# Recurrence of a two-block transformer kernel: the first chunk products of two of the four chains are issued in the input stages

## The chip, the cores and the metric

The kernel runs on one core of one Trainium2 chip, in one launch. The metric is the device time of the launch in microseconds (us). Five engines work side by side and meet at semaphores: TensorE (PE in the profile, with its weight loads as PEld), VectorE (DVE), ScalarE (ACT), GpSimd (POOL) and the queue of SyncE (SP), which issues most transfers.

## The reference, cut to what matters

Two transformer blocks over 256 tokens of width 1024. The second block holds a gated linear recurrence over 8 heads of size 64, run forward and backward in time, once over a context of 256 tokens (only the last state is needed) and once over the tokens themselves:

```
def step(S, inp):
    w_t, k_t, v_t, a_t, b_t = inp[:5]
    sa = jnp.einsum('bhij,bhj->bhi', S, a_t)
    S = S * w_t[:, :, None, :] + sa[..., None] * b_t[:, :, None, :] + v_t[..., None] * k_t[:, :, None, :]
    y = jnp.einsum('bhij,bhj->bhi', S, inp[5]) if emit else None
    return S, y
```

After it come a merge with a convolution branch, and a mixture of 16 experts whose weights are most of the bytes that the kernel reads.

## The kernel before, in words

The kernel does not step through the tokens. It cuts the 256 tokens into 8 chunks of 32 (`CH`), and solves each chunk with small matrix products. `recurrence_phase` runs twice: for the context (names begin with `rc`, `ctx_only` is true) and for the tokens (`rl`). Each run has two directions, d = 0 and d = 1, and for each direction two stages, one behind the other: `recurrence_inputs` and `recurrence_chunks`. That makes four pairs of stages: rc0, rc1, rl0, rl1. Each stage is a block of its own: every engine waits at its end for the others, and GpSimd clears the semaphores of the stage, one after another, before it goes on.

**The input stage** makes the scaled factors. DVE writes `ar[:, :, 0]` (L2683), `bk[:, :, 0]` (L2688), `bk[:, :, 1]` (L2691), and for the tokens `ar[:, :, 1]` (L2698). `ebk[:, 0]` is made on POOL (L2644) and `ebk[:, 1]` on DVE (L2695). One semaphore, `ready`, counts the three that are to be transposed: 1 for `ar` from DVE, 2 for `ebk[:, 0]` from POOL, 3 for `ebk[:, 1]` from DVE. DVE waits for `ready` to be 2 before it makes `ebk[:, 1]`, so that the count has one meaning. PE transposes each in two groups of four 128x128 tiles (L2605), `j` counting the tensors (0 is `v`), into two PSUM banks in turn, and ACT copies each group out (L2631). PE also does a matrix product for a later stage in pieces (L2097, `LateModulation`), and where d is 1 it carries the states of the direction before (`States`, L3070 to L3084), with DVE adding between them (L3100). Behind DVE's products, POOL keeps the keys for the tokens (L2649, L2651).

**The chunk stage** works on four chains, q = 0 to 3, each half of the tokens and half of the heads. `order()` goes through 13 rounds r, and in each through the four chains. In round 0, PE makes the raw products of a chain: 32 matmul instructions for the context and 48 for the tokens, each 64 rows deep with 32 columns of weights (L2831, L2833, L2835, L2837). A profile shows each of them as two matmul records and two weight loads, because they are float32. DVE then masks them (L3006) and spreads them (L3008), ACT copies four corners (L2929) and writes `off` (L2934), into buffers that POOL has set to zero (L2957, L2958). Rounds 1 and later multiply, spread and combine. PE starts round 1 of a chain when DVE and ACT have done its round 0.

PSUM has eight banks. Chain q uses banks 2q and 2q + 1. In the input stage the small products of the decay and the rate use banks 2 to 5 (L2582, L2584), the transposes banks 6 and 7 where d is 0 and 2 and 3 where d is 1, the states banks 0, 1 and 6, and the piecewise product bank 0 or 7.

Of the kernel before, what the change touches and what calls it, by code (L numbers as in the profile page):

```python
# [8 lines left out]
P = 128  # L9
# [2526 lines left out]


def recurrence_inputs(nc, g, I, z, ar, bk, tok, pc, store, part, st, ctx_only, name, d):

# [3 lines left out]
    with ExitStack() as ctx:  # L2543
# [34 lines left out]
        @block.tensor  # L2578
        def _(pe):
            pe.wait_ge(g.lora_in, 32 * lora_loads)  # L2580
            for c in range(PAIRS):
                nc.tensor.matmul(ps[:, 2 + c // 2, T * (c % 2):T * (c % 2) + T], g.lora[0:64, P * c:P * c + P],  # L2582
                                 z[0:64, 12, :], start=True, stop=True).then_inc(S["lora_w"], 1)
                mm = nc.tensor.matmul(ps[:, 4 + c // 2, T * (c % 2):T * (c % 2) + T], g.lora[64:P, P * c:P * c + P],  # L2584
                                      z[64:P, 12, :], start=True, stop=True)
            mm.then_inc(S["lora"], 1)
            if d:
                for n in range(NCH):
                    before.pe_step(pe, n)
                    for k in range(2 * n, min(2 * n + 2, KC)):  # L2590
                        late.pe_step(pe, k)

            q = 0
            for j in range(d, 4):
                if j == 1 and d == 0:
                    for k in range(KC):
                        late.pe_step(pe, k)
                if j:
                    pe.wait_ge(S["ready"], j)
                for t in range(TT):  # L2600
                    if q >= 2:
                        pe.wait_ge(S["tokcopy"], q - 1)
                    for c in range(PAIRS):
                        src = (v_[:, c], ar[:, c, 0], ebk[:, 0, c], ebk[:, 1, c])[j][:, P * t:P * t + P]
                        mm = nc.tensor.transpose(ps[:, turn0 + q % 2, P * c:P * c + P], src, g.ident[:])  # L2605
                    mm.then_inc(S["tokturn"], 1)
                    q += 1
# [28 lines left out]
        def _(pool):  # L2636
            p_ = nc.gpsimd
            for c in range(PAIRS):
# [5 lines left out]
            p_.tensor_tensor(chunked(ebk[:, 0]), chunked(bk[:, :, 0, :]), pc[:].unsqueeze(3).to_broadcast([P, PAIRS, NCH, CH]),  # L2644
                             ALU.mult).then_inc(S["ready"], 1)
            if not ctx_only:
# [8 lines left out]
        def _(dve):  # L2655
# [12 lines left out]
            for c in range(PAIRS):  # L2668
                dve.wait_ge(S["log"], c + 1)
                ins = v.tensor_tensor_scan(onward(cum[:, c, :]), g.restart[:], onward(ld[:, c, :]), 0.0, ALU.mult, ALU.add)  # L2670
                if c == 1:
# [18 lines left out]
            dve.wait_ge(S["keys"], 1)  # L2690
            ch(v.tensor_tensor(bk[:, :, 1, :], keys[:], shrunk[:], ALU.mult))  # L2691
            move_state()
            dve.wait_ge(S["exp"], 3)
            dve.wait_ge(S["ready"], 2)
            v.tensor_tensor(chunked(ebk[:, 1]), chunked(bk[:, :, 1, :]), pc[:].unsqueeze(3).to_broadcast([P, PAIRS, NCH, CH]),  # L2695
                            ALU.mult).then_inc(S["ready"], 1)
            if not ctx_only:
                ch(v.tensor_tensor(ar[:, :, 1, :], r, grown[:], ALU.mult))  # L2698
            if d and not ctx_only:
# [8 lines left out]
def recurrence_chunks(nc, g, ar, bk, tok, pc, store, part, ctx_only, name, d):  # L2708
# [6 lines left out]
    with ExitStack() as ctx:  # L2715
# [57 lines left out]
        def g2c(q):  # L2773
            return pair[:, q, 1]

        def order():
            for r in range(CHUNK_ROUNDS):
                for q in range(len(its)):
                    yield q, r

        def group(i):
            return slice(CH * i, CH * i + CH)
# [25 lines left out]
        def _(pe):  # L2808
# [9 lines left out]
            for q, r in order():  # L2818
                (t, h4), out = its[q], bank(q, r)
                by_dve, by_act = S[f"by_dve{q}"], S[f"by_act{q}"]  # L2820
                if r == 0:
                    for k in range(2):
                        for kind in range(2 if ctx_only else 3):
                            for c in range(4):
                                for e in range(2):
                                    half, pr = slice(HD * e, HD * e + HD), 2 * h4 + k
                                    tok_c = slice(P * t + CH * c, P * t + CH * c + CH)
                                    a, bb = ar[half, pr, :, tok_c], bk[half, pr, :, tok_c]
                                    out = ps[group(c), 2 * q + e, 256 * k:256 * k + n_raw]
                                    if kind == 0:  # L2830
                                        mm = mm_(out[:, 0:64], a[:, 0], bb[:, 0:2], start=True, stop=True)  # L2831
                                    elif ctx_only:
                                        mm = mm_(out[:, 64:96], bb[:, 0], a[:, 0], start=True, stop=True)  # L2833
                                    elif kind == 1:
                                        mm = mm_(out[:, 64:128], bb[:, 0], a[:, 0:2], start=True, stop=True)  # L2835
                                    else:
                                        mm = mm_(out[:, 128:160], bb[:, 1], a[:, 1], start=True, stop=True)  # L2837
                elif r == 1:
# [36 lines left out]
                elif r == 5:  # L2875
                    pe.wait_ge(by_dve, FACTOR)
                    if not ctx_only:
                        pe.wait_ge(S["joined"], q + 1)
                    for hs in range(4):
# [10 lines left out]
                elif r == 8:  # L2890
                    pe.wait_ge(by_dve, FTIL)
                    pe.wait_ge(S["read_out"], q + 1)
                    for hs in range(4):
                        mm = by_pairs(out, hs, read_out(q)[:, hs], ftil(q)[:, hs])
                else:
# [4 lines left out]
                    else:  # L2900
                        pe.wait_ge(S[f"pe{q}"], r)
                    for k in range(2):
# [13 lines left out]
        def _(act):  # L2916
# [3 lines left out]
            for q, r in order():  # L2920
                (t, h4), done = its[q], S[f"by_act{q}"]
                if r in (4, 7, 8, 9, 11, 12):
                    continue
                act.wait_ge(S[f"pe{q}"], r + 1)
                if r == 0:
                    act.wait_ge(S["zeros"], q + 1)
                    act.wait_ge(S[f"by_dve{q}"], RAW)
# [26 lines left out]
        def _(pool):  # L2954
            tt, copy, zero = nc.gpsimd.tensor_tensor, nc.gpsimd.tensor_copy, nc.gpsimd.memset
            for q in range(NQ):
                zero(off[:, q], 0.0)  # L2957
# [6 lines left out]
            def join(q):  # L2964
                t, h4 = its[q]
                pool.wait_ge(S[f"pe{q}"], 3)
                kt = tok[:, 1, t, 256 * h4:256 * h4 + 256].rearrange("p (k e n) -> p e k n", k=2, e=2)
                copy(f1(q)[:, :, 0:HD].rearrange("p (e k) n -> p e k n", e=2), kt)
                copy(f1(q)[:, :, HD:wide], raw[:, q, :, 96:128]).then_inc(S["joined"], 1)

            for q in range(NQ):
                expand(q)
            if not ctx_only:
                for q in range(NQ):
                    join(q)
            for q in range(NQ):
                pool.wait_ge(S[f"pe{q}"], 5)
                tt(in_halves(read_out(q)), twice(raw[:, q, :, CH:2 * CH]), own_half, ALU.mult).then_inc(S["read_out"], 1)
# [3 lines left out]
            if not ctx_only:  # L2982
                for q, (t, h4) in enumerate(its):
                    pool.wait_ge(S[f"by_dve{q}"], G2)
# [6 lines left out]
        def _(dve):  # L2991
# [8 lines left out]
            for q, r in order():  # L3000
                (t, h4), done = its[q], S[f"by_dve{q}"]
                if r in (5, 6, 9, 10, 11):
                    continue
                dve.wait_ge(S[f"pe{q}"], r + 1)
                if r == 0:
# [10 lines left out]
                elif r == 2:  # L3016
                    spread_low(q, r).then_inc(done, 1)
                    dve.wait_ge(S[f"by_act{q}"], HIGH + 1)
                    dve.wait_ge(S["expanded"], q + 1)
                    dve.wait_ge(S["minus"], 1)  # L3020
# [894 lines left out]
```

## Time and profile before

| What | Value |
|---|---|
| Median of 3 runs | 2251.73 us (2250.79 to 2252.65) |
| Span of the profiled execution | 2252.5 us |
| Instructions | 36461 |
| PE busy | 1746.6 us (78%) |
| PE weight loads busy | 1172.5 us (52%) |
| DVE busy | 826.5 us (37%) |
| ACT busy | 652.2 us (29%) |
| POOL busy | 230.2 us (10%) |
| Read from the chip's main memory | 584.88 MB |

The span is the time from the first to the last instruction of one profiled execution; only the span is shown for that execution, and it lies within the three times. Busy shares are averages over a whole program with very different stages, so they say little about the recurrence. The four pairs of stages lie at these times of the span: rc0 from 801 to 858 us, rc1 from 858 to 918, rl0 from 1035 to 1099, rl1 from 1099 to 1171.

### The profile page before, as it was taken

How to read it: one execution, taken by the hardware profiler on the slowest of the kernel's cores; microseconds unless marked ns; L12 is line 12 of the kernel's file. 1: busy time of each engine (PE TensorE's matmuls, PEld its weight loads, DVE VectorE, ACT ScalarE, POOL GpSimd, SP SyncE). 2: the span in 40 equal slices, each digit the busy share in tenths (PEclk: the TensorE clock that was granted, in tenths of full speed). 3: DMA queues.
4: the chain of work that ended last, by engine and by line, in shares of the span. 5: the costliest groups of instructions: out<-in, count | busy, mean ns of one | idle time of the engine just before them, and what ended most of it. 6: DMA issues, size and time to landing. Idle time of an engine off the chain costs nothing. (4 is left out here: it accounts for less than half of the span.)

```text
span 2252.5 us, 36461 instructions
## 1 busy us (share of the span) xinstructions
PE 1746.6 (78%) x15950; PEld 1172.5 (52%) x15950; DVE 826.5 (37%) x1187; ACT 652.2 (29%) x1053; POOL 230.2 (10%) x222
## 2 busy tenths in 40 slices
PE   7999988979999977897889976556566666565654
PEld 7997986867878855796779741111111111111111
DVE  5654445765755666675656540000000000000001
ACT  5434445564423455444453320000000000000001
POOL 0100014430121032002330000000000000000000
PEclk9999998999999989897979988887778877778787
DMA  7654652235855522253215579999999999999997
GB/s 234 188 187 150 206 161 64 88 129 189 279 162 191 182 92 78 73 178 100 66 41 206 204 279 428 429 428 428 428 428 428 428 428 428 428 428 428 427 427 305
DMA packets 181906, 588.39 MB, mean 261 GB/s; under 512 B 11363, under 2 KB 144166, under 8 KB 156918
## 3 DMA queue, kind: packets, MB, share of 16 engines
q1 hardware_dynamic: 180550, 585.32, 67.6%
q8 instruction: 126, 2.06, 0.4%
q10 hardware_dynamic: 1200, 0.76, 0.1%
q14 instruction: 30, 0.25, 0.0%
HBM read 584.88 MB, written 1.17 MB: 260 GB/s over the span
## 5 line engine op out<-in xcount | busy, mean ns | idle before, releaser
L193 DVE TENSOR_TENSOR split_lo<-ring,split_hi 128x2048 fp32r<-128x2048 f32 x127 | 295.8, 2331 | 193.6 <-ACT split_hi L186 192.9
L3659 PE MATMUL ps<-ex_ring,ex_xe 128*32 128x512 f32 x1440 | 233.5, 783 | 157.0 <-DMA ex_ring<-in_exp_w 157.0
L3740 DVE TENSOR_TENSOR ex_hid<-ps,ex_silu 128x512 f32<-128x512 f32 x16 | 11.1, 692 | 863.1 <-PE ps L3659 863.1
L221 PE MATMUL ps<-xt_hi,split_hi 128*128 128x256 f32 x984 | 284.4, 289 | 13.0 <-DVE xt_lo L350 5.3
L186 ACT CAST split_hi<-ring 128x2048 fp32r<-128x2048 f32 x127 | 240.4, 1897 | 144.1 <-PE ps L223 123.5
L222 PE MATMUL ps<-xt_lo,split_hi 128*128 128x256 f32 x984 | 279.2, 284 | 0.0
L223 PE MATMUL ps<-xt_hi,split_lo 128*128 128x256 f32 x984 | 279.0, 284 | 0.0
L3659 PEld LDWEIGHTS ps<-ex_ring,ex_xe 128*32 128x32 f32 x1440 | 45.1, 128 | 342.0 <-DMA ex_ring<-in_exp_w 246.7
L221 PEld LDWEIGHTS ps<-xt_hi,split_hi 128*128 128x128 f32 x984 | 188.5, 192 | 24.9 <-issue 14.3
L222 PEld LDWEIGHTS ps<-xt_lo,split_hi 128*128 128x128 f32 x984 | 188.5, 192 | 1.2 <-issue 1.2
L221 PE MATMUL ps<-split_hi,xt_hi 128*128 128x256 f32 (+1 forms) x560 | 175.6, 314 | 16.7 <-DVE split_lo L193 7.1
L223 PEld LDWEIGHTS ps<-xt_hi,split_lo 128*128 128x128 f32 x984 | 188.4, 191 | 0.0
L222 PE MATMUL ps<-split_lo,xt_hi 128*128 128x256 f32 (+1 forms) x560 | 174.4, 312 | 0.0
L223 PE MATMUL ps<-split_hi,xt_lo 128*128 128x256 f32 (+1 forms) x560 | 173.8, 310 | 0.0
L3681 PE MATMUL ps<-ex_ring,ex_ht 128*32 128x512 f32 x688 | 112.1, 783 | 72.7 <-DMA ex_ring<-in_exp_w 66.0
L221 PEld LDWEIGHTS ps<-split_hi,xt_hi 128*128 128x128 f32 x560 | 107.3, 192 | 25.2 <-DVE split_lo L193 5.8
L223 PEld LDWEIGHTS ps<-split_hi,xt_lo 128*128 128x128 f32 x560 | 107.1, 191 | 6.3
L222 PEld LDWEIGHTS ps<-split_lo,xt_hi 128*128 128x128 f32 x560 | 107.3, 192 | 5.8
L3659 PE MATMUL ps<-ring,ex_xe 128*32 128x512 f32 x416 | 65.5, 762 | 47.2 <-DMA ring<-in_exp_w 45.6
L3681 PEld LDWEIGHTS ps<-ex_ring,ex_ht 128*32 128x32 f32 x688 | 21.6, 129 | 149.4 <-DMA ex_ring<-in_exp_w 98.0
L3700 ACT COPY ex_wselt<-ps 128x256 f32<-128x256 f32 x16 | 6.0, 373 | 294.8 <-PE ps L3665 294.8
L3698 ACT ACTIVATE ex_silu<-ps 128x512 f32<-128x512 f32 x16 | 9.6, 597 | 276.3 <-PE ps L3659 276.3
(766 smaller groups left out, 2811.5 us busy)
## 6 DMA issues: line engine op xcount, KB each, us to landing
ex_ring<-in_exp_w SPq DMA_DIRECT2D x133, 2048.0 KB, 46.0
ring<-in_exp_w SPq DMA_DIRECT2D x39, 2048.0 KB, 46.0
ring<-in_w_in SPq DMA_DIRECT2D x55, 1024.0 KB, 5.3
ex_late<-in_exp_w SPq DMA_DIRECT2D x18, 2048.0 KB, 46.2
ring<-in_ffn_w_gate SPq DMA_DIRECT2D x22, 1024.0 KB, 6.0
ring<-in_ffn_w_up SPq DMA_DIRECT2D x22, 1024.0 KB, 5.5
ring<-in_ffn_w_down SPq DMA_DIRECT2D x22, 1024.0 KB, 4.9
ring<-in_mod_w SPq DMA_DIRECT2D x16, 1024.0 KB, 6.5
```

What stands on the lines that cost most here:

```text
L186: nc.scalar.copy(g.whi[:, s % H, 0:n], g.ring[:, i % R, 0:n]).then_inc(g.hi_done, 1)
L193: eng.tensor_tensor(g.wlo[:, s % H, 0:n], g.ring[:, i % R, 0:n], g.whi[:, s % H, 0:n].bitcast(F32), ALU.subtract).then_inc(g.tiles_split, 1)
L221: nc.tensor.matmul(out, lhs[0], rhs[0], start=start, stop=False, skip_group_check=shared)
L222: nc.tensor.matmul(out, lhs[0], rhs[1], start=False, stop=False, skip_group_check=shared)
L223: return nc.tensor.matmul(out, lhs[1], rhs[0], start=False, stop=stop, skip_group_check=shared)
L3659: mm = mm_(ps[32 * q:32 * q + 32, 4 + u, :], xe[:, k], w[:, 512 * q:512 * q + 512], start=k == 0, stop=k == KC - 1)
L3681: mm = mm_(ps[32 * q:32 * q + 32, 7, :], ht[:, 2 * (k % 2) + h, CAP * f:CAP * f + CAP], w[:, h, 512 * n:512 * n + 512], start=k == 0, stop ...
L3698: nc.scalar.activation(silu[:], ps[:, 4, :], ACT.Silu).then_inc(S["silu"], 1)
L3700: nc.scalar.copy(wselt[:], ps[:, 6, 0:T]).then_inc(S["wselt"], 1)
L3740: v.tensor_tensor(hid[:], ps[:, 5, :], silu[:], ALU.mult).then_inc(S["hid"], 1)
```

## The change

Four things are changed.

1. The raw products of round 0 become a function, `first_products`. For two of the four chains (1 and 2 where d is 0, 2 and 3 where d is 1) it is called in the input stage, before the transposes of `ebk[:, 0]` and of `ebk[:, 1]`, and no longer in the chunk stage. Their banks are free of the input stage's own work by then.
2. A new semaphore, `factors`, is raised once both halves of `bk` (and for the tokens both of `ar`) are written. PE waits for it before the first of these calls. For the tokens, DVE makes `ar[:, :, 1]` before `ebk[:, 1]` and not after it.
3. `ready` is split in three, so that DVE makes `ebk[:, 1]` without waiting for POOL's `ebk[:, 0]`.
4. In the chunk stage the two early chains come first in each round, on every engine, and the waits count their PE rounds from round 1.

```diff
+EARLY = {0: (1, 2), 1: (2, 3)}
+def first_products(nc, g, ar, bk, ctx_only, q):
...
     (in recurrence_inputs, tensor)
+                if j >= 2:
+                    if j == 2:
+                        pe.wait_ge(S["factors"], 1)
+                        pe.wait_ge(S["log"], PAIRS)
+                        pe.wait_ge(S["rate"], PAIRS)
+                    elif d:
+                        pe.wait_ge(S["state"], before.moves + 1)
+                        pe.wait_ge(g.mod_copied, late.n + 1)
+                    first_products(nc, g, ar, bk, ctx_only, EARLY[d][j - 2])
                 if j:
-                    pe.wait_ge(S["ready"], j)
+                    pe.wait_ge(S[("", "ready", "ready_b", "ready_k")[j]], 1)
...
     (in recurrence_inputs, vector)
             dve.wait_ge(S["keys"], 1)
-            ch(v.tensor_tensor(bk[:, :, 1, :], keys[:], shrunk[:], ALU.mult))
+            if not ctx_only:
+                ch.add(v.tensor_tensor(bk[:, :, 1, :], keys[:], shrunk[:], ALU.mult))
+                v.tensor_tensor(ar[:, :, 1, :], r, grown[:], ALU.mult).then_inc(S["factors"], 1)
+            else:
+                ins = v.tensor_tensor(bk[:, :, 1, :], keys[:], shrunk[:], ALU.mult)
+                ins.then_inc(S["factors"], 1)
             move_state()
+            dve.wait_ge(S["factors"], 1)
             dve.wait_ge(S["exp"], 3)
-            dve.wait_ge(S["ready"], 2)
             v.tensor_tensor(chunked(ebk[:, 1]), chunked(bk[:, :, 1, :]), pc[:].unsqueeze(3).to_broadcast([P, PAIRS, NCH, CH]),
-                            ALU.mult).then_inc(S["ready"], 1)
-            if not ctx_only:
-                ch(v.tensor_tensor(ar[:, :, 1, :], r, grown[:], ALU.mult))
+                            ALU.mult).then_inc(S["ready_k"], 1)
...
     (in recurrence_chunks)
+        early = EARLY[d]
+        chains = [*early, *(q for q in range(NQ) if q not in early)]
         def order():
             for r in range(CHUNK_ROUNDS):
-                for q in range(len(its)):
+                for q in chains:
                     yield q, r
...
                 if r == 0:
+                    if q in early:
+                        continue
+                    mm = first_products(nc, g, ar, bk, ctx_only, q)
```

The body of `first_products` is the loop of round 0, moved without an edit. The lines in brackets say where a piece stands.

## Rows read from the trace of the kernel before

**Rows 1.** Page, part 4: the chain that ended last, share of the span by engine.
```profile
DMA 37%; PE 3%; DVE 0%; ACT 0%; SPq 0%; issue 0%; DVEq 0%
```

**Rows 2.** Windows: from:to, length, busy (records) by engine, PE first, clock, DMA share, GB/s.
```profile
1055.50:1100.00 44.50, 34.97 (x1250) 31.44 (x1252) 25.56 (x53) 22.54 (x66) 19.12 (x32) 0.81 0.05 14
...
1059.60:1061.65 2.05, 2.03 (x128) 0.50 0.03 8
...
1063.10:1065.70 2.60, 2.60 (x128) 0.50 0.02 6
...
821.75:823.70 1.95, 1.91 (x176) 1.00 1.10 347
```

**Rows 3.** Timeline of PE, rl0: start, us, operation, and in brackets idle before and releaser.
```profile
1050.06 4.03 PE L2605 MATMUL ps<-ident,rl0i_ebk 128*128 128x128 f32 x16 [2.07 <-POOL rl0i_ebk L2644]
1055.53 0.47 PE L2831 MATMUL ps<-rl_bk,rl_ar 64*32 64x64 f32 x16 [1.45 <-PEq L2543]
...
1059.62 0.21 PE L2837 MATMUL ps<-rl_ar,rl_bk 64*32 64x32 f32 x1 [1.96 <-issue]
```

**Rows 4.** Timeline of ACT, first copies of round 0 and of round 1, rl0.
```profile
1058.03 1.22 ACT L2929 COPY rl0c_both<-rl0c_raw 32x128 f32<-32x128 f32 x4 [1.89 <-DVE rl0c_raw L3006]
...
1067.91 0.74 ACT L2939 COPY rl0c_both<-ps 32x256 f32<-32x256 f32 x2
```

**Rows 5.** Timeline of ACT, the same in rc0, rc1 and rl1.
```profile
823.53 1.22 ACT L2929 COPY rc0c_both<-rc0c_raw 32x128 f32<-32x128 f32 x4 [1.14 <-POOL rc0c_both L2958]
...
830.92 4.57 ACT L2939 COPY rc0c_both<-ps 32x256 f32<-32x256 f32 x12
...
882.67 1.22 ACT L2929 COPY rc1c_both<-rc1c_raw 32x128 f32<-32x128 f32 x4 [1.28 <-POOL rc1c_both L2958]
...
889.36 5.39 ACT L2939 COPY rc1c_both<-ps 32x256 f32<-32x256 f32 x14
...
1139.76 0.74 ACT L2939 COPY rl1c_both<-ps 32x256 f32<-32x256 f32 x2
```

**Rows 6.** Timeline of POOL, second half of the first chain's zeros in rl0.
```profile
1057.02 0.53 POOL L2958 MEMSET rl0c_both<- 128x512 f32 x1
```

**Rows 7.** Timeline of DVE and of POOL, input stage of rl0.
```profile
1047.02 1.22 DVE L2691 TENSOR_TENSOR rl_bk<-rl0i_keys,rl0i_shrunk 128x1024 f32<-128x1024 f32 x1
1050.14 1.92 DVE L2695 TENSOR_TENSOR rl0i_ebk<-rl_bk,rl_pc 128x1024 f32<-128x1024 f32 x1 [1.91 <-POOL rl0i_ebk L2644]
...
1047.18 2.82 POOL L2644 TENSOR_TENSOR rl0i_ebk<-rl_bk,rl_pc 128x1024 f32<-128x1024 f32 x1 [3.68 <-DVE rl_bk L2688]
```

**Rows 8.** Timeline of DVE, of POOL and of PE, input stage of rl1.
```profile
1118.96 2.52 DVE L2691 TENSOR_TENSOR rl_bk<-rl1i_keys,rl1i_shrunk 128x1024 f32<-128x1024 f32 x1
...
1120.37 3.35 POOL L2651 TENSOR_TENSOR kmod_y<-kmod_y,rl1i_keys 128x1024 f32<-128x1024 f32 x1
...
1124.85 1.09 PE L2605 MATMUL ps<-ident,rl1i_ebk 128*128 128x128 f32 x8 [1.54 <-DVE rl1i_ebk L2695]
1127.76 0.47 PE L2831 MATMUL ps<-rl_bk,rl_ar 64*32 64x64 f32 x16 [1.82 <-PEq L2543]
```

**Rows 9.** Timelines of PE in rc0, then of DVE and PE in rc1, input stages.
```profile
816.50 3.79 PE L2605 MATMUL ps<-ident,rc0i_ebk 128*128 128x128 f32 x16 [2.82 <-POOL rc0i_ebk L2644]
...
873.67 2.83 DVE L2691 TENSOR_TENSOR rc_bk<-rc1i_keys,rc1i_shrunk 128x1024 f32<-128x1024 f32 x1
...
876.06 3.28 PE L2605 MATMUL ps<-ident,rc1i_ebk 128*128 128x128 f32 x16
```

**Rows 10.** Timeline of DVE and POOL elsewhere: two products in a row against one of POOL.
```profile
500.92 3.59 DVE L193 TENSOR_TENSOR split_lo<-ring,split_hi 128x2048 fp32r<-128x2048 f32 x1
...
499.95 2.41 POOL L1521 TENSOR_TENSOR proj<-proj 128x1024 f32<-128x1024 f32 x1 [26.19 <-DVE proj L1543]
```

**Rows 11.** Timeline of DVE and POOL in rl1: two scans in a row against one operation of POOL.
```profile
1104.46 1.29 DVE L2670 TENSOR_TENSOR_SCAN rl1i_cum<-restart,rl1i_ld 128x256 f32<-128x256 f32 x2
...
1104.77 1.18 POOL L2640 TENSOR_SCALAR rl1i_keys<-rl1i_av,vb,one_minus_ka 128x256 f32<-128x256 f32 x1 [10.49 <-ACT rl1i_av L2617]
```

## Prediction before the run

> **What bounds the kernel now.** I read the page first. The chain that ended last is 37% DMA and 3% PE [rows 1]: from the experts on, the kernel waits for weights. That stream starts only after the recurrence, the merge and the router, and its loads are issued as those stages free their buffers. So a microsecond won or lost in the recurrence moves the stream by as much, and I carry it over at full value.
>
> Then I read the timelines of each engine in the four pairs of stages, because shares of busy time say nothing about stages that wait for one another. Three things stand out.
>
> First, PE in round 0 of a chunk stage is not held by a semaphore but by "issue". In rl0 it stood still for 1.96 us until 1059.62, then ran exactly 128 records, stood still, and ran 128 again [rows 2, 3]. The runs of 128 begin 3.5 us apart (1059.60 and 1063.10). One matmul record goes with one weight load, so a run is 256 instructions. The reading: instructions arrive in blocks of 256, one is executed while the next one is there, and the block after that is asked for when a block is finished; it takes 3.5 us or more. Where the matmuls are small, PE eats a block in 2.05 us at the half clock (0.50) and then waits. The Trainium skill (Runtime: NRT & Kernel Launch, Instruction fetch mechanics) also has blocks of 256 instructions, but gives PE room for 2048 and calls the crossing mostly hidden. By that the stalls would not be there, and my sum would be about 1 us lower, since I count one such stall in rl1. The trace disagrees: PE stops after every 128 records.
>
> Second, round 0 sets the start of everything else. ACT copies the corners of all four chains before it may touch round 1. In rc1 these copies ran without a gap, from 882.67 to 889.36 [rows 5], 6.7 us for four chains. In rl0 they took from 1058.03 to 1067.91 [rows 4], since each waited for raw products.
>
> Third, DVE and POOL hold each other up. POOL's `ebk` product took 2.82 us in rl0 beside a DVE product that started before it [rows 7]; DVE's product took 2.52 us in rl1 instead of 1.22 [rows 7, 8].
>
> **What the chunk stages gain.** The removed work is round 0 of two chains, out of the way before the stage begins. DVE can mask them at once, and the two chains left are made meanwhile. What sets the end of round 0 is then ACT: its start plus 6.7 us. Its start needs zeros from POOL, which in rl0 came at 1057.02 + 0.53 = 1057.55, that is 2.0 us after the stage began at 1055.53 [rows 3, 6]. POOL clears three semaphores more in each input stage (`factors`, `ready_b`, `ready_k`). Their clears are not in the rows; POOL needs less than 1.5 us from the start of the stage to its zeros, for 14 semaphores, so three more cost at most 0.3 us; I take 0.2.
> - rl0: before, round 1 on ACT began 1067.91 - 1055.53 = 12.4 us into the stage. After: 2.0 + 0.1 + 0.2 + 6.7 = 9.0. Gain 3.4.
> - rl1: before 1139.76 - 1127.76 = 12.0 [rows 5, 8]; after 9.0. Gain 3.0.
> - rc0: before, 830.92 - 821.8 = 9.1, with ACT already released by POOL at 823.53 [rows 2, 5]. After: 1.7 + 0.2 + 6.7 = 8.6. Gain 0.5.
> - rc1: ACT was already without a gap behind POOL's zeros [rows 5]. Nothing to gain; the clears cost 0.2.
>
> Sum of gains: 3.4 + 3.0 + 0.5 - 0.2 = 6.7 us. From round 1 on every instruction stands at the same place in PE's stream, so I take the rest as shifted and unchanged.
>
> **What the input stages lose.** PE stands idle before `ebk[:, 0]` only: 2.07 us in rl0, 2.82 in rc0 [rows 3, 9]. The call before `ebk[:, 1]` has no such cover, since the transposes run in one piece of four groups. The price of a call: 64 records for the context, 96 for the tokens, at 2.05 / 128 = 16 ns a record at the half clock, 1.95 / 176 = 11 ns at full [rows 2]. So 0.7 to 1.0 us, and 1.05 to 1.5 us. Two groups of transposes took 1.09 us at full clock (rl1) and 4.03 / 2 = 2.0 us in rl0 [rows 3, 8]. After the last transpose, copy and barrier took 1055.53 - 1054.09 = 1.44 us.
> - rc0: the first call runs while PE waits for POOL and is free. The second costs 0.7 to 1.0. If the call keeps the clock up, the transposes, 3.79 us here [rows 9], would go in 2.2, a gain. Bounds -0.9 and +1.0; I take +0.8, nearest to the rows.
> - rc1: before, the transposes started at 876.06 and ended at 879.34. Now the first call waits for `bk`, ready at 873.67 + 2.83 = 876.50 [rows 9]. Then 0.7, 1.1, 0.7, 1.1: end at 880.1, at the half clock in part 881. ACT's copies, which paced the transposes before, hide behind the calls. +0.8 to +1.7; I take +1.2.
> - rl0: the call needs `ar[:, :, 1]` too, which DVE now makes right behind `bk[:, :, 1]`, in the time when POOL's `ebk` product waits for the shared path. Who goes first? Elsewhere DVE ran, straight behind another product, one over 2048 columns in 3.59 us, where 1024 columns take 1.22 alone [rows 7], so some 2.4 were due; a product of POOL that was issued before it took 2.41 us and ended 1.4 us into it [rows 10]: POOL got in between. So POOL runs until 1050.0, DVE until 1051.1, and the call starts at 1051.15 and not at 1049.4. Then call, two groups, call, two groups: 1.5 + 2.0 + 1.5 + 2.0 = 7.0 at the half clock, end 1058.15 against 1054.09, +4.1. At full clock it is 1.05 + 1.1, then the second call meets a block that was asked for at 1051.5 and comes 3.7 us later, then 0.4 and 1.1: 1056.8, +2.7. PE will be denser than before, so I take +3.5.
> - rl1: `bk` is ready at 1121.48. POOL's `kmod` product has waited since 1120.37 and ran until 1123.72 [rows 8]; by the same order `ar[:, :, 1]` runs after it, until 1124.8. PE has nothing else to do by then and stands still. Call 1.05, two groups 1.1, then the second call stalls for its block (asked for at 1125.4, there at 1129.1), 0.2, and two groups 1.1 to 2.0: end 1130.4 to 1131.3. Before: 1125.94. The stage ended then 1.8 us after it, as DVE copied outputs, and now 1.44. +4.1 to +5.0; I take +4.4.
>
> Sum of losses: 0.8 + 1.2 + 3.5 + 4.4 = 9.9 us. Dropping DVE's wait for POOL gains nothing by itself: both want the same path, and PE is not waiting for `ebk[:, 1]` any more.
>
> **Sum.** 9.9 - 6.7 = +3.2 us: rc0 +0.3, rc1 +1.4, rl0 +0.1, rl1 +1.4. The profiled execution spans 2252.5 us, within the three runs, so on the median 2251.7 + 3.2 = 2254.9 us. A difference of under 0.2% (4.5 us) is about what a measurement of this kernel can't tell from none.
>
> **Rivals.**
> - *DVE keeps the path between two products in a row.* Two scans did: a POOL operation issued during the first took 1.18 us and ended after the second, which was not slowed (the two took 1.29) [rows 11]. Then `factors` comes at 1049.4 and 1122.6. rl0 costs 1.5 us less, rl1 2.5 less: -0.8, 2250.9 us. The Trainium skill (SBUF — State Buffer, two separate sides) says that whichever starts first holds the pair for the whole instruction, which agrees with rows 7 and leaves open who is next. Chance 0.20.
> - *Instruction blocks bind the whole chunk stage (the faster side).* A chunk stage for the tokens has some 1250 records, 9.8 blocks, at 3.5 us 34 us of its 44. If the blocks set the pace past round 1, moving 1 block out of each context stage and 1.5 out of each token stage saves 2 x 3.5 + 2 x 5.2 = 17.5 us instead of 6.7: 2251.7 + 9.9 - 17.5 = 2244 us. It decides from the point where PE waits for "issue" in late rounds; in rl0 the waits of that kind that I found are in round 0 and the first of round 1. Chance 0.10.
> - *Blocks come late while weights are loaded.* Weights of later stages load during the input stages; where such a load still ran, the DMA share was 1.10 [rows 2]. The fetches inside the input stages were hidden, so their length there is unknown. If one takes 6 us instead of 3.7, each second call ends some 2 us later: +4 to +5, 2259 us. Chance 0.15.
>
> **How the numbers follow.** The forecast has 0.55; its own range is 2251 to 2258, with a third of it above the 0.2% line. Slower: 0.18 from it and 0.14 of the late blocks, 0.32. Faster: the block rival, 0.10. Same: 0.58. The range 2249 to 2260 leaves out the block rival and the far end of the late ones.
>
> **What would show it.** In the changed kernel: PE's wait for `factors` ends at DVE's `ar` product in rl0 and rl1, some 3 us after `bk` starts in rl0; a wait on "issue" inside the second call of rl1; input stages longer by about 1, 1, 3.5 and 4.5 us; ACT's copies of round 0 without a gap, 6.7 us in all four; chunk stages for the tokens shorter by about 3 us. Wrong if DVE's `ar` product is not held up, if the clock rises in the input stages, or if late rounds of the chunk stages shrink too.

## The result

The changed kernel is slower: 2261.34 us median of 20 runs, against 2255.33 us of the kernel before in 20 runs beside them. The two medians lie 6.0 us apart; the ratio of the fast runs, which leaves out two of the kernel before at 4029 and 5836 us, is 1.0035 [1.0027, 1.0043], some 8 us. The profiled executions say much the same: span 2259.8 us against 2252.5, +7.3. The forecast was +3.2 us, 2254.9 (from a median of three runs that lay 3.6 us below that of the twenty), with a range to 2260, which the median passes by 1.3 us. The direction was right and the size, by the ratio, less than half of what came.

I cut each pair of stages at three events of ACT: its first activation of the input stage, the start of the chunk stage, and its first copy of round 1. "Rest" runs from there to the next stage. In us, worked out from ACT's timeline, one profiled execution each:

| | input stage: before, after, forecast | round 0: before, after, forecast | rest: before, after, forecast |
|---|---|---|---|
| rc0 | 18.24, 18.85: +0.6, +0.8 | 9.16, 8.63: -0.5, -0.5 | 29.73, 30.49: +0.8, 0 |
| rc1 | 20.11, 20.94: +0.8, +1.2 | 8.60, 8.77: +0.2, +0.2 | 27.40, 27.92: +0.5, 0 |
| rl0 | 18.39, 24.32: **+5.9, +3.5** | 12.40, 8.98: -3.4, -3.4 | 33.85, 34.13: +0.3, 0 |
| rl1 | 25.97, 31.95: **+6.0, +4.4** | 12.03, 8.91: -3.1, -3.0 | 31.68, 32.20: +0.5, 0 |

From the start of rc0 to the merge the kernel took 367.92 us before and 375.76 after, +7.8. It is made up of +13.3 in the input stages, -6.9 in round 0, +2.1 in the rests, and -0.7 in the work between rc1 and rl0. After the merge both need the same time (1081.1 and 1081.3).

### The profile page after: what moved, and what is told of

Its sections match the earlier page's. It is cut to its first block and busy times, and to the rows that moved or that the text cites. A ratio compares the mean times of both kernels' runs of the same rounds, so it can differ in the third digit from the quotient of the medians.

```text
span 2259.8 us, 36476 instructions
## 1 busy us (share of the span) xinstructions
PE 1752.3 (78%) x15950; PEld 1177.2 (52%) x15950; DVE 829.6 (37%) x1187; ACT 651.3 (29%) x1053; POOL 231.0 (10%) x222
## 5 line engine op out<-in xcount | busy, mean ns | idle before, releaser
L221 PE MATMUL ps<-xt_hi,split_hi 128*128 128x256 f32 x984 | 284.7, 289 | 13.3 <-DVE xt_lo L350 5.6
L221 PEld LDWEIGHTS ps<-xt_hi,split_hi 128*128 128x128 f32 x984 | 188.6, 192 | 25.2 <-issue 14.4
L3716 PE MATMUL ps<-ex_ring,ex_ht 128*32 128x512 f32 x688 | 116.9, 813 | 77.9 <-DMA ex_ring<-in_exp_w 73.2
```

The costliest lines, as they stand in the source:

```text
L221: nc.tensor.matmul(out, lhs[0], rhs[0], start=start, stop=False, skip_group_check=shared)
L3716: mm = mm_(ps[32 * q:32 * q + 32, 7, :], ht[:, 2 * (k % 2) + h, CAP * f:CAP * f + CAP], w[:, h, 512 * n:512 * n + 512], start=k == 0, stop ...
```

## The profile after

The chain that ended last still waits for weights, as in [rows 1]:

```profile
DMA 37%; PE 3%; DVE 0%; ACT 0%; issue 0%; DVEq 0%
```

DVE and POOL in the input stage of rl0 (start, us, instruction, idle before and releaser), which answer to [rows 7]:

```profile
1047.64 1.22 DVE L2727 TENSOR_TENSOR rl_bk<-rl0i_keys,rl0i_shrunk 128x1024 f32<-128x1024 f32 x1
1048.78 2.94 DVE L2728 TENSOR_TENSOR rl_ar<-z,rl0i_grown 128x1024 f32<-128x1024 f32 x1
1051.75 1.94 DVE L2735 TENSOR_TENSOR rl0i_ebk<-rl_bk,rl_pc 128x1024 f32<-128x1024 f32 x1
...
1047.82 2.82 POOL L2679 TENSOR_TENSOR rl0i_ebk<-rl_bk,rl_pc 128x1024 f32<-128x1024 f32 x1 [3.68 <-DVE rl_bk L2723]
```

DVE's `ar[:, :, 1]` was issued behind `bk[:, :, 1]` and took 2.94 us in place of 1.22: POOL's product, which had waited since 1047.82, went in between. `factors` came at 1051.72. The stages ahead had moved all of this by 0.62 us (1047.64 against 1047.02), so it came at 1051.1 on the clock of before, which is the forecast.

PE in the same stage, the answer to [rows 3]:

```profile
1051.77 0.47 PE L2554 MATMUL ps<-rl_bk,rl_ar 64*32 64x64 f32 x16 [4.03 <-DVE rl_ar L2728]
...
1053.21 1.96 PE L2640 MATMUL ps<-ident,rl0i_ebk 128*128 128x128 f32 x8
1055.10 0.34 PE L2554 MATMUL ps<-rl_bk,rl_ar 64*32 64x64 f32 x16
...
1055.60 0.28 PE L2554 MATMUL ps<-rl_bk,rl_ar 64*32 64x64 f32 x4
1058.33 0.28 PE L2554 MATMUL ps<-rl_bk,rl_ar 64*32 64x64 f32 x5 [2.45 <-issue]
...
1058.99 1.97 PE L2640 MATMUL ps<-ident,rl0i_ebk 128*128 128x128 f32 x8
1062.38 0.47 PE L2554 MATMUL ps<-rl_bk,rl_ar 64*32 64x64 f32 x16 [1.42 <-PEq L2569]
```

The first call takes 1.4 us, its two groups of transposes 1.9. The second call gets through 55 records and stops for "issue", that is for instructions. Counted back from the stop, 128 records are those 55, the 8 transposes, and 65 of the 96 of the first call, so the block in use began at its 32nd record, at about 1052.2. By the prediction's reading the next block was asked for then. It was there at 1058.33: 6.1 us, where the forecast had 3.7. All lengths of a fetch in this document are counted this way. The windows (length, busy and records of PE, PEld, DVE, ACT, POOL, granted clock, DMA share, GB/s) show what else went on:

```profile
1051.80:1053.20 1.40, 1.40 (x96) 1.35 (x96) 1.40 (x1) 0.00 (x0) 0.81 (x1) 0.50 1.10 347
1053.20:1055.20 2.00, 2.00 (x27) 1.67 (x27) 0.49 (x1) 0.59 (x1) 0.00 (x0) 0.54 1.10 349
1055.20:1058.50 3.30, 0.85 (x75) 0.70 (x82) 0.00 (x0) 0.59 (x1) 0.00 (x0) 0.99 1.01 326
1058.50:1061.00 2.50, 2.45 (x49) 1.99 (x35) 0.00 (x0) 0.60 (x2) 0.00 (x0) 0.50 0.06 20
```

Weights of a later stage load at 326 to 349 GB/s until just before the block is there. In rl1 there is the same stop, with a difference:

```profile
1128.13 0.35 PE L2554 MATMUL ps<-rl_bk,rl_ar 64*32 64x64 f32 x16 [2.92 <-DVE rl_ar L2728]
...
1129.18 1.09 PE L2640 MATMUL ps<-ident,rl1i_ebk 128*128 128x128 f32 x8
...
1133.60 0.31 PE L2558 MATMUL ps<-rl_ar,rl_bk 64*32 64x64 f32 x1 [2.42 <-issue]
...
1134.05 1.97 PE L2640 MATMUL ps<-ident,rl1i_ebk 128*128 128x128 f32 x8
```

```profile
1128.70:1131.30 2.60, 2.48 (x146) 2.10 (x132) 1.96 (x5) 1.07 (x2) 0.00 (x0) 1.00 1.09 342
1131.30:1133.60 2.30, 0.00 (x1) 0.00 (x1) 0.00 (x0) 0.00 (x0) 0.00 (x0) 0.99 0.05 16
```

By the same count (78 records of the second call, 8 transposes, 42 of the first call) the block in use began at about 1128.7, and the next took 4.9 us. Here the loads were over at about 1131.3, and the block came 2.3 us after that. PE came out of the wait, did a fifth of a call, and had its last two groups at the half clock (1.97 us, against 1.09 for the two before).

The chunk stage of rl0 on ACT, the answer to [rows 4]:

```profile
1064.64 1.22 ACT L2963 COPY rl0c_both<-rl0c_raw 32x128 f32<-32x128 f32 x4 [1.66 <-POOL rl0c_both L2992]
1065.88 0.52 ACT L2968 ACTIVATE rl0c_off<-ps,halves 128x64 f32<-128x64 f32 x2
1066.29 1.20 ACT L2963 COPY rl0c_both<-rl0c_raw 32x128 f32<-32x128 f32 x4
...
1071.33 0.74 ACT L2973 COPY rl0c_both<-ps 32x256 f32<-32x256 f32 x2
```

ACT is released by POOL's zeros, 2.26 us into the stage (1064.64 - 1062.38; forecast 2.0 + 0.1 + 0.2), and then copies all four chains without a gap, 6.69 us (forecast 6.7).

## The experiments

Each kernel was timed in five rounds against the kernel before on the same chip, 6 to 12 executions against 22 to 35; ratios are against that, and the row "after" repeats the result. The columns of stages are, for rl0 and rl1, input stage / round 0 / rest, in us, each from one profiled execution:

| kernel | ratio | rl0 | rl1 | rc0 to merge |
|---|---|---|---|---|
| before | 1 | 18.4 / 12.4 / 33.9 | 26.0 / 12.0 / 31.7 | 367.9 |
| after | 1.0035 [1.0027, 1.0043] | 24.3 / 9.0 / 34.1 | 32.0 / 8.9 / 32.2 | 375.8 |
| e1_loads_later | 1.0049 [1.0035, 1.0063] | 21.5 / 9.0 / 34.0 | 30.4 / 8.9 / 34.9 | 377.4 |
| e2_none_early | 1.0016 [1.0005, 1.0028] | 19.1 / 12.3 / 33.8 | 29.4 / 11.5 / 31.7 | 371.4 |
| e3_context_only | 1.0028 [1.0016, 1.0039] | 19.2 / 12.7 / 34.0 | 27.1 / 12.3 / 32.0 | 372.2 |
| e4_tokens_only | 1.0022 [1.0011, 1.0033] | 24.1 / 9.0 / 33.8 | 31.7 / 8.9 / 32.0 | 372.6 |
| e5_one_call | 0.9995 [0.9985, 1.0005] | 19.6 / 9.7 / 33.3 | 29.5 / 8.9 / 31.9 | 367.2 |
| e6_ar_first | 1.0030 [1.0020, 1.0040] | 21.9 / 9.0 / 33.9 | 32.7 / 8.9 / 32.0 | 372.9 |
| e7_tokens_one_free | 0.9989 [0.9977, 1.0001] | 18.9 / 9.0 / 33.6 | 27.0 / 9.8 / 32.5 | 365.6 |
| e8_before_keys_last | 0.9994 [0.9982, 1.0007] | 18.0 / 12.4 / 33.3 | 25.2 / 11.5 / 32.3 | 366.2 |
| e9_two_calls_free | 1.0022 [1.0012, 1.0032] | 22.8 / 9.0 / 33.6 | 33.8 / 8.9 / 31.7 | 372.4 |
| e10_one_call_free | 0.9995 [0.9986, 1.0004] | 18.9 / 9.0 / 33.4 | 26.8 / 9.8 / 32.0 | 363.6 |
| e11_before_loads_later | 1.0078 [1.0063, 1.0092] | 18.1 / 16.3 / 35.0 | 26.3 / 15.3 / 33.1 | 382.7 |

### e1_loads_later: is the block late because of the weights?

The changed kernel, with the loads of the late weight tiles issued in the following chunk stage and not in the input stage:

```diff
-            late.load_next(sp)                 (input stage, sync)
+        load_tiles(g, sp, ... + 4 + R)         (chunk stage, sync)
```

> The changed kernel, with SyncE's loads of the next four weight tiles moved from the input stages into the chunk stages that follow. Theory 1 (a block of instructions comes late because it queues behind weight loads): PE's wait on issue inside the second call of rl0 and rl1, 2.7 us each in the changed kernel, shrinks to 1 us or less, the input stages of rl0 and rl1 end some 2 us earlier each, and the time falls by 3 to 5 us against the changed kernel, to +2 to +5 us against the kernel before. Theory 2 (a fetch takes its 6 us whatever else is moved): the waits stay at 2.5 us and more, and the time stays at about +8 us.

The input stages got shorter, by 2.9 us in rl0 and 1.6 in rl1. In rl0 the second call starts at 1056.73 and its transposes follow at 1058.17, 1.44 us later, with no wait on "issue" in it:

```profile
1056.73 0.47 PE L2554 MATMUL ps<-rl_bk,rl_ar 64*32 64x64 f32 x16
...
1058.17 1.15 PE L2640 MATMUL ps<-ident,rl0i_ebk 128*128 128x128 f32 x8
```

PE's instructions are those of the changed kernel, so a block ends at the same record. In rl0 that is the 56th of the second call, some 3.7 us after the block began, and the next one was there. In rl1 it is the 79th, and PE's weight loads stop there for only 0.27 us:

```profile
1130.90 0.22 PEld L2558 LDWEIGHTS ps<-rl_ar,rl_bk 64*32 64x32 f32 x13
1131.38 0.10 PEld L2558 LDWEIGHTS ps<-rl_ar,rl_bk 64*32 64x32 f32 x1 [0.27 <-issue]
```

The block in use had begun at 1127.90, so this fetch took 3.5 us, and 4.9 with the loads beside it. Theory 1 holds for the stages: a block comes late because of the loads. The time did not fall with it, as theory 1 had it: it is 1.0049, some 3 us above the changed kernel (the intervals overlap) and not 3 to 5 below. The rest of the chunk stages grew by 1.9 us (rc0), 0.7 (rc1) and 2.7 (rl1) over the changed kernel, where the loads now run beside the chunk stage's blocks: one fetch took 7.3 us in rl0 and one 6.8 in rl1. I had not seen that the loads must be somewhere.

### e11_before_loads_later: the same move in the kernel before

> The kernel before with the loads of the late weight tiles moved from the input to the following chunk stage. Theory (a block of instructions comes late while weights load): the input stages, where fetches lie under other waits, stay within 0.5 us, and the chunk stages grow by 1 to 3 us in rc0 and rl1 as they did with the same move in the changed kernel; time 2255 to 2258 us. Rival (the chunk stages grew for another reason in that version): chunk stages within 0.5 us, time the same as before.

The stage changed, and the size was wrong: input stages within 0.7 us, chunk stages 2.0 (rc0) and 4.4 us (rc1) longer, those of the tokens 5.0 (rl0) and 4.7 us (rl1), there mostly in round 0. The kernel was 0.78% slower, some 17.6 us and not 2 to 5. PE in round 0 of rl0:

```profile
1062.54 0.32 PE L2831 MATMUL ps<-rl_bk,rl_ar 64*32 64x64 f32 x13 [1.42 <-PEq L2543]
1066.76 0.21 PE L2837 MATMUL ps<-rl_ar,rl_bk 64*32 64x32 f32 x1 [2.68 <-issue]
1073.24 0.26 PE L2835 MATMUL ps<-rl_ar,rl_bk 64*32 64x64 f32 x1 [4.46 <-issue]
```

and what the window of that stretch holds:

```profile
1063.00:1073.00 10.00, 3.11 (x238) 2.79 (x234) 2.84 (x4) 3.55 (x13) 3.82 (x10) 0.59 0.99 319
```

The same code as in [rows 2, 3], whose runs of 128 records began 3.5 us apart, has them 6.5 us apart (1066.76, 1073.24) when weights load at 319 GB/s. This is the price of a block by itself, without any of the change: 3.5 us in a quiet stage, 6.5 beside weight loads. Over the thirteen traces, the fetches inside one stage that PE had to wait for took 2.9 to 4.4 us with the DMA share under 0.1 and 5.8 to 7.3 us with it above 0.9. Some that run over the end of an input stage don't fit: the one after the stop in rl1 of the changed kernel took 7.2 us, from 1133.60 to 1140.81, at a DMA share of 0.01. Why is open.

### e2, e3 and e4: the change in parts

e2_none_early keeps DVE's order and the split `ready` and issues no call early; e3_context_only has the calls of rc0 and rc1, e4_tokens_only those of rl0 and rl1.

```diff
+def EARLY_OF(ctx_only, d):
+    return ()                              (e2)
+    return EARLY[d] if ctx_only else ()    (e3)
+    return () if ctx_only else EARLY[d]    (e4)
```

> The changed kernel without the early calls: all four chains have round 0 in the chunk stage, in the old order; DVE's new order and the split of the ready semaphore stay. If the early calls carry the loss, it is gone: -1 to +1 us against the kernel before. If the order on DVE (ar behind bk, held up by POOL) costs by itself, +1 to +3 us are left.

> Early calls in the two context pairs only. By the two traces the context pairs lost 0.9 and 1.5 us (input stages +0.6 and +0.8, chunk stages +0.2 and +0.7): +2 to +3 us against the kernel before. By the prediction's sum they lose 1.7. A rival: all of the loss of the late blocks sits in the token pairs and the context pairs are within 1 us of the kernel before.

> Early calls in the two token pairs only. By the two traces rl0 and rl1 lost 2.7 and 3.8 us (input stages +6, chunk stages -3): +5 to +7 us against the kernel before. By the prediction's sum +1.5. Together with the context-only kernel it should add up to the whole change, +8 us.

By the stages, e3's context pairs lost 2.2 us and e4's token pairs 5.1. As whole kernels they are some 6.3 and 5.0 us slower than before: e3 lies above the +2 to +3 that had been expected, since e2's part is in it, and e4 at the low end of its range. The ratios add up: 1.0028 and 1.0022, less the 1.0016 that both contain, make 1.0034; each is known to 0.0012, so this is no sharp test. The surprise is e2. DVE's order and the split semaphore alone, with no product moved, cost 0.16%, some 3.6 us (1.1 to 6.3). Its rl1 on DVE, to be read beside [rows 8]:

```profile
1117.13 2.52 DVE L2731 TENSOR_TENSOR rl_bk<-rl1i_keys,rl1i_shrunk 128x1024 f32<-128x1024 f32 x1
1119.57 3.38 DVE L2732 TENSOR_TENSOR rl_ar<-z,rl1i_grown 128x1024 f32<-128x1024 f32 x1
1122.99 1.23 DVE L2739 TENSOR_TENSOR rl1i_ebk<-rl_bk,rl_pc 128x1024 f32<-128x1024 f32 x1
```

POOL's keys stand between `bk` and the next product of DVE in both kernels. Before, that next product was `ebk[:, 1]`, which PE needs; now it is `ar[:, :, 1]`, and `ebk[:, 1]` follows 1.2 us later. Counted from the start of `bk[:, :, 1]`, the rest of the stage was 1.0 us (rl0) and 0.9 us (rl1) longer than before, in e2 and in e3 alike: that is the price of the order, 1.9 us, within the +1 to +3 that had been expected. The input stage of rl1 as a whole was 3.4 us longer in e2. The other 2.5 had come before `bk[:, :, 1]`, while PE carried the states at the half clock, where in the kernel before it did so at the full one (windows of e2, then of the kernel before):

```profile
1099.04:1104.90 5.86, 5.86 (x70) 3.98 (x68) 1.76 (x3) 3.79 (x8) 2.99 (x4) 0.51 0.00 0
1103.39:1107.90 4.51, 4.51 (x90) 3.40 (x89) 2.67 (x5) 3.79 (x8) 2.79 (x4) 1.00 0.00 0
```

PE had no idle time in either. Why the clock rose later in e2 isn't known, and one execution doesn't tell whether it always does, so part of the 0.16% may be this and not the order.

e4 pays the whole price in the token stages that the changed kernel pays (+5.7 and +5.7 in the input stages) and gets the same round 0.

### e6_ar_first: take DVE's product out of the wait

The changed kernel, with `ar[:, :, 1]` made before `bk[:, :, 0]`, when POOL has nothing to run:

```diff
+            if not ctx_only:
+                ch.add(v.tensor_tensor(ar[:, :, 1, :], r, grown[:], ALU.mult))
             v.tensor_tensor(bk[:, :, 0, :], rated[:], shrunk[:], ALU.mult)...
-                v.tensor_tensor(ar[:, :, 1, :], r, grown[:], ALU.mult)...
```

> The changed kernel with DVE making ar[:, :, 1] before bk[:, :, 0] in the token pairs, where no POOL product is waiting. Theory (POOL holds up ar by its length): DVE's product takes 1.2 us and not 2.9 and 3.4, factors comes 1 to 2 us earlier in rl0 and 2 us earlier in rl1, and the time falls by 1 to 4 us against the changed kernel. Rival: the late block sets the end of the stage, then the block, asked for earlier, is as much earlier too, or waits for the loads anyway: then only 0 to 1 us.

`ar[:, :, 1]` took 1.22 us, and the first call of rl0 no longer waited for it. The input stage of rl0 was 2.4 us shorter than in the changed kernel, that of rl1 0.8 longer, and the time is as good as unchanged (1.0030 against 1.0035, some 1 us), as the rival had it. The profiled execution took 2.9 us less from rc0 to the merge, but it is the fastest of the twelve, 4.5 us under their median. In rl0 the call starts 1.7 us earlier in the stage and the wait for the block is no longer (2.02 us, 2.45 in the changed kernel). In rl1 it starts only 0.8 us earlier, and the wait grows from 2.42 to 4.01 (rl0, then rl1):

```profile
1046.69 0.47 PE L2554 MATMUL ps<-rl_bk,rl_ar 64*32 64x64 f32 x16 [2.43 <-DVE rl_bk L2728]
...
1053.49 0.26 PE L2554 MATMUL ps<-rl_bk,rl_ar 64*32 64x64 f32 x5 [2.02 <-issue]
...
1121.29 0.35 PE L2554 MATMUL ps<-rl_bk,rl_ar 64*32 64x64 f32 x16 [0.49 <-DVE rl_bk L2728]
...
1128.35 0.31 PE L2558 MATMUL ps<-rl_ar,rl_bk 64*32 64x64 f32 x1 [4.01 <-issue]
```

### e5, e7 and e10: one early chain in each pair

`EARLY[d][:1]` in place of `EARLY[d]`, so that the call before the last transposes is gone. e5 does that in all four pairs. e7 does it for the tokens alone, with `ar` first, and POOL keeps its keys back until `ebk[:, 1]` is made:

```diff
                 pool.wait_ge(S["keys"], 1)
+                pool.wait_ge(S["ready_k"], 1)
```

e10 is e7 with the context's calls as well.

> The changed kernel with one early chain in each pair (1 or 2), called before the transposes of ebk[:, 0]; the second call is gone. If the second call, with its late block of instructions, carries the loss of the input stages, those of rl0 and rl1 end 3 to 5 us earlier than in the changed kernel, those of the context pairs 1 us, while round 0 in the token pairs takes about 1 us longer: 0 to +3 us against the kernel before. If the first call, late for its factors, carries it, +5 us and more are left.

> A version built from the readings: early calls in the token pairs only, one chain, DVE makes ar[:, :, 1] first, and POOL keeps the keys only when ebk[:, 1] is made. Expected from the rows: rl0 -1 to -2.5 us, rl1 -2 to -3 us, context 0: -3 to -5 us against the kernel before. If chip executions differ by more than that through the clock, it cannot be told from 0.

> One early chain in each of the four pairs, ar[:, :, 1] before bk[:, :, 0] and POOL's keys behind ebk[:, 1]: the parts that measured well, together. Theory: the sum of what they gave, rc0 and rc1 as in the version with one call (-0.2 and +1.4 us on before by the traces), rl0 -3 and rl1 0 to -1: 2249 to 2251 us, ratio 0.998 to 0.999. Rival (gains of this size are placement of instruction blocks and not the edits): within 0.1% of before, and the stages without an edit move as much as those with one.

e5 is the largest step of the study: 0.9995, from 1.0035, by leaving one call out. The input stage of rl0 was 4.7 us shorter than in the changed kernel, that of rl1 2.5 (3 to 5 had been expected), that of rc0 0.8, that of rc1 no shorter. Round 0 hardly noticed: 9.7 us in rl0 and 8.9 in rl1, where two calls gave 9.0 and 8.9. In e7, rl0's input stage is 0.5 us longer than before and its round 0 is 9.0: nearly all of the gain of 3.4 us, for nearly nothing. PE in that stage:

```profile
1047.53 0.47 PE L2558 MATMUL ps<-rl_bk,rl_ar 64*32 64x64 f32 x16 [2.44 <-DVE rl_bk L2733]
1049.30 3.82 PE L2644 MATMUL ps<-ident,rl0i_ebk 128*128 128x128 f32 x16 [0.26 <-POOL rl0i_ebk L2683]
1054.56 0.32 PE L2558 MATMUL ps<-rl_bk,rl_ar 64*32 64x64 f32 x13 [1.44 <-PEq L2573]
1058.54 0.24 PE L2562 MATMUL ps<-rl_ar,rl_bk 64*32 64x64 f32 x1 [2.12 <-issue]
```

The call lies wholly in PE's wait for POOL. A block still comes late, at 1058.54, but inside round 0, where ACT is busy with the chains that are there.

e7 had been expected 3 to 5 us under the kernel before and came to 2.5 under it, with 0 in its interval; rl1, expected 2 to 3 us shorter, was 0.4 shorter. e10 had been expected at 2249 to 2251 us and came to 2251.88. No version is faster than the kernel before beyond its interval. From rc0 to the merge e7 took 2.4 us less and e10 4.4 us less than before, by one profiled execution each; after the merge they took 2.3 and 2.5 us more (1083.3 and 1083.6 against 1081.1). Kernels that differ in nothing after the merge had 1079.9 to 1083.6 there, so a gain of this size is not to be told from chance.

### e9_two_calls_free: the second call by itself

e7 with both calls; the two differ in the second call alone.

> As e7_tokens_one_free, but both early chains of the tokens, so that the second call's price is measured with the shared path free. Theory (the second call pays for a late instruction block and buys nothing, because the second chain's raw products are made anyway while DVE and ACT work on the first): input stages 3 us (rl0) and 4 to 6 us (rl1) longer than with one call, round 0 at 9.0 us in both; time some 7 us over that of one call, 2256 to 2260 us. Rival (the second call was only dear because of the held-up products): inputs within 1.5 us of those with one call, round 0 shorter by 0.5 us, time within 2 us of it.

The theory held. The input stages took 4.0 us (rl0) and 6.8 us (rl1) more, a little over what was expected. Of the 6.8, 1.6 had come before the first call, with PE at the half clock for the first 6 us of that stage, 2 us longer than in e7. Counted from the first call, the second cost 3.6 us in rl0 and 5.2 in rl1, and round 0 took 0.0 and 0.9 less: 8.9 us paid for 0.9. From rc0 to the merge it was 6.8 us more, since round 0 of rc0 and some of the rests of that execution were shorter, and the time, 2257.33 us, is in the range that was expected. PE in rl1:

```profile
1123.74 0.35 PE L2558 MATMUL ps<-rl_bk,rl_ar 64*32 64x64 f32 x16 [0.49 <-DVE rl_bk L2733]
1124.80 1.09 PE L2644 MATMUL ps<-ident,rl1i_ebk 128*128 128x128 f32 x8
...
1130.74 0.21 PE L2562 MATMUL ps<-rl_ar,rl_bk 64*32 64x64 f32 x1 [3.95 <-issue]
1130.97 1.63 PE L2644 MATMUL ps<-ident,rl1i_ebk 128*128 128x128 f32 x8
```

The call waits 3.95 us for its block here, and waited 2.42 in the changed kernel. The fetch took 6.5 us here, with loads beside it for 4.4, and 4.9 there, with loads beside it for 2.6. So in rl1 an earlier call meets more of the loads and waits longer. In rl0 it doesn't: the wait was 1.80 us in e9 and 2.02 in e6, against 2.45.

### e8_before_keys_last: POOL's keys alone

The kernel before, with one line, `pool.wait_ge(S["ready"], 3)`, ahead of POOL's keys.

> The kernel before, with one edit: POOL keeps the keys only when ebk[:, 1] is made. Theory (DVE and POOL take turns, and POOL's long product comes first in rl1): DVE's ebk product takes 1.2 us and not 3.3, and the input stage of rl1 ends 1 to 1.5 us earlier: 0 to -1.5 us, too small to be told in the time, but plain in the rows.

DVE's `ebk[:, 1]` took 1.23 us in rl1 and not 3.27. The input stage was 0.8 us shorter (1.1 counted from the start of `bk[:, :, 1]`), a little short of what was expected, the time the same within its interval.

## Why the prediction was right in direction and short in size

**Round 0** was right in all four pairs, to 0.1 us: the zeros, three more clears, and 6.7 us of copies. For rc0 that is in part luck: with no early chain its round 0 took 8.7 to 9.4 us in e4, e7, e8 and e9, so a gain of 0.5 is not clear of what executions differ by.

**The shared path of DVE and POOL** was right: `ar[:, :, 1]` was held up in both token stages, and `factors` came when the forecast had it, also in rl1: 1128.07, less the 3.3 us by which the stage had moved (DVE's `bk[:, :, 1]` at 1122.26 against 1118.96), is 1124.8. The rival in which DVE keeps the path (0.20) is ruled out.

**The failed step is the length of a block's fetch in the input stages of the tokens**: "a block that was asked for at 1051.5 and comes 3.7 us later", and the same 3.7 in rl1. The 3.7 was taken from chunk stages, where the DMA engines stand nearly still; the calls were to run in stages where weights load. It took 6.1 us in rl0 and 4.9 in rl1; e1, the same calls without the loads, had 3.5 in rl1 and no more than 3.7 in rl0, and e11 measured 6.5 in place of 3.5 with the loads as the only difference. The rival "blocks come late while weights are loaded" had this mechanism and this length (6 us) at a chance of 0.15, and its time, 7.3 us above the median shown of before, is close to what came; the row it rested on, a DMA share of 1.10 in such a stage, was the evidence for giving it more. This accounts for +2.4 us in rl0 and +1.2 in rl1, of the +2.4 and +1.6 by which the forecast fell short there, and for most of the 4.6 us by which it fell short from rc0 to the merge (7.8 against 3.2). The Trainium skill (Runtime: NRT & Kernel Launch, Instruction fetch mechanics) calls such crossings mostly hidden. Here one was hidden in e1, where transposes stood between two calls and no weights loaded; where small matmuls follow one another or weights load, waits of 2 to 4.5 us stand in the rows.

**The clock** took some of it too. The forecast for rl0 weighed a half-clock case without a stall (+4.1) and a full-clock case with one (+2.7). Both came at once: the granted clock was 0.50 (1.2 GHz) in the first call and 0.54 in the transposes behind it, 0.99 while PE stood in the stall, and 0.50 again in the last transposes, in rl1 as well, where all had run at 1.00 (2.4 GHz) before the stall. The +3.5 taken between the two cases is also what rl0 comes to without its wait of 2.45 us; that is luck.

**"Shifted and unchanged"** was off by 2.1 us in the sum of the four rests. Its cause stays open. The rest of rc0 was 30.4 us in e2 and in e8, where its chunk stage has no early chain, and 29.5 to 29.9 in e4, e7 and e9, where it has none either; a term of this size in one profiled execution is within what such versions differ by. The other way went the 0.7 us that the work between rc1 and rl0 was shorter, as it was in most versions.

**What the chance should have been asked of** is the second call. The prediction priced it as a cost and never asked what it buys. It buys nothing in rl0 (9.0 us with one call in e7, 9.0 with two in e9) and 0.9 us in rl1, since the other chains' products are made while ACT works on the first.

## What to carry to other kernels

Before work is moved into a gap, ask of each piece what the consumer waits for with one piece less: here one chain was enough to start ACT, and with the second left out no loss was left that the runs could tell. A run of small matmuls costs its instruction blocks as well as its time, and the price of a block is to be read in a stage with the same load on the DMA queues as the one it is moved to. A product that two engines compete for is best placed where the other has nothing to run: `ar[:, :, 1]` took 1.22 us there in place of 2.9 and 3.4, though the time hardly moved (e6).

## What the runs showed of the hardware

- A block of 256 instructions of PE (128 matmul records and their weight loads, which are 64 float32 matmuls of the program) reached it 3.5 us after the one before in a quiet stage and 6.5 us after it beside weight loads at 319 GB/s (e11). In round 0 of rl0 a run of 128 records took 2.05 us at the half clock, and the next run began 3.5 us after the start of the first.
- A product of POOL on two tensors that was waiting got in between two products of DVE that followed one another without a gap, in both token stages and in each kernel with that order: 2.93 to 2.94 us in rl0 and 3.36 to 3.38 in rl1, where 1.22 is the time alone. The two scans of [rows 11] had kept POOL out; what makes the difference wasn't tried.
- Moving weight loads (four of 1 MB each in rl0) from under DVE's work to under PE's small matmuls cost the kernel before some 17.6 us (0.78%), with nothing added to the work of any engine.
